# A hybrid decoder trunk on one core: the state-space sums moved behind the fifth step's value products, and a compression on two column groups

## The reference

```python
# NSA: overlapping blocks of 32 tokens, every 16, are compressed to one key and one value each
nc = S // CMP_STRIDE - 1                                   # 15 blocks
def compress(t, pe, w):
    ch = t.reshape(B, S // CMP_STRIDE, CMP_STRIDE, d)
    blk = jnp.concatenate([ch[:, :-1], ch[:, 1:]], axis=2)
    return ((blk + pe).reshape(B, nc, CMP_LEN * d) @ w).astype(F32)
kc = compress(keys[:, :, 0], cmp_pe[0], w_cmp[0])          # d = 64
vc = compress(vals[:, :, 0], cmp_pe[1], w_cmp[1])
# SSD: running sums of the decay within and over chunks of 128 tokens
a_cs = jnp.cumsum(a, axis=-1)
Lm = jnp.exp(segsum(a))
scores = jnp.einsum('bclhn,bcshn->bhcls', Cc, Bc) * Lm
y_diag = jnp.einsum('bhcls,bcshp->bclhp', scores, x)
```

## Time and profile before

| | us |
|---|---|
| median of three runs | 1509.21 (1509.17 to 1509.39) |
| the profiled execution, its own time | 1509.64 |
| its span in the trace | 1507.9 |
| TensorE busy | 1486.9 (99% of the span) |
| VectorE busy | 1213.4 (80%) |
| ScalarE busy | 1000.3 (66%) |
| mixers' loop, layer 0 / layer 1 | about 80 to 137 / 457 to 514 |

### The profile page before, as it was taken

One profiled execution on the slowest core, in us unless ns is written; L12 is line 12 of the kernel. 1 busy time (PEld: TensorE's weight loads), 2 busy tenths in 40 slices (PEclk: granted clock), 3 DMA queues, 4 the chain that ended last, 5 costly groups with the idle time before them and its releaser, 6 DMA issues.

```text
span 1507.9 us, 20053 instructions
## 1 busy us (share of the span) xinstructions
PE 1486.9 (99%) x7413; PEld 1245.8 (83%) x7413; DVE 1213.4 (80%) x1283; ACT 1000.3 (66%) x894; POOL 82.7 (5%) x126
## 2 busy tenths in 40 slices
PE   9999999999999999999999999999999999999997
PEld 7987888888898888888888888888888888888885
DVE  7778545545577899989898899898988899889986
ACT  7376543444547577787777777777777777778765
POOL 3102000000000110000000000000000000000000
PEclk9999999999999999999999999999999999999999
DMA  9705655555530379999999999999999999999992
GB/s 319 249 2 131 240 176 195 194 195 170 190 115 2 112 274 396 396 354 394 395 346 394 394 356 384 394 380 357 396 394 345 394 396 342 395 396 344 393 396 87
DMA packets 189980, 444.23 MB, mean 295 GB/s; under 512 B 9729, under 2 KB 16014, under 8 KB 189918
## 3 DMA queue, kind: packets, MB, share of 16 engines
q1 hardware_dynamic: 185366, 427.81, 77.5%
q0 software_dynamic: 4528, 15.58, 3.9%
q10 hardware_dynamic: 24, 0.01, 0.0%
HBM read 435.51 MB, written 7.86 MB: 294 GB/s over the span
## 4 chain that ended last, share of the span: by engine, by line
PE 94%; DVE 2%; ACT 2%; issue 1%; POOL 0%; SPq 0%; DMA 0%; POOLq 0%; DVEq 0%; ACTq 0%
PE bank L478 27%; PE bank L479 27%; PE bank L477 27%; PE bank L618 3%; PE bank L540 2%; PE bank L732 1%; PE bank L621 1%; PE bank L780 1%; PE bank L749 1%; PE bank L790 0%; PE bank L1020 0%; DMA ring<-in_w_in_dram 0%; POOL rstd L1303 0%; PE bank L650 0%; PE bank L713 0%
## 5 line engine op out<-in xcount | busy, mean ns | idle before, releaser
L1909 DVE TENSOR_TENSOR w_lo<-ring,w_hi 128x2048 fp32r<-128x2048 f32 x372 | 846.4, 2290 | 176.1 <-ACT w_hi L1427 175.6
L1427 ACT ACTIVATE w_hi<-ring 128x2048 fp32r<-128x2048 f32 x372 | 712.2, 1917 | 221.7 <-PE bank L477 221.7
L478 PE MATMUL bank<-w_hi,xT_hi 128*128 128x512 f32 x896 | 353.5, 395 | 0.0
L479 PE MATMUL bank<-w_hi,xT_lo 128*128 128x512 f32 x896 | 349.4, 390 | 0.0
L477 PE MATMUL bank<-w_lo,xT_hi 128*128 128x512 f32 x896 | 240.2, 390 | 0.0
L478 PE MATMUL bank<-w_hi,hidT_hi 128*128 128x512 f32 x560 | 220.6, 394 | 0.0
L479 PE MATMUL bank<-w_hi,hidT_lo 128*128 128x512 f32 x560 | 218.2, 390 | 0.0
L477 PEld LDWEIGHTS bank<-w_lo,xT_hi 128*128 128x128 f32 x896 | 168.1, 188 | 36.0 <-DVE w_lo L1909 0.3
L479 PEld LDWEIGHTS bank<-w_hi,xT_lo 128*128 128x128 f32 x896 | 168.3, 188 | 33.9
L478 PEld LDWEIGHTS bank<-w_hi,xT_hi 128*128 128x128 f32 x896 | 168.3, 188 | 33.6
L478 PE MATMUL bank<-w_hi,hT_hi 128*128 128x512 f32 (+2 forms) x384 | 147.3, 387 | 4.8 <-DVE hT_lo L1864 2.7
(11 more groups left out here) (393 smaller groups left out, 1269.6 us busy)
## 6 DMA issues: line engine op xcount, KB each, us to landing
ring<-in_moe_w_gate_dram SPq DMA_DIRECT2D x112, 1024.0 KB, 9.4
ring<-in_moe_w_up_dram SPq DMA_DIRECT2D x112, 1024.0 KB, 9.4
ring<-in_moe_w_down_dram SPq DMA_DIRECT2D x112, 1024.0 KB, 9.1
ring<-in_ffn_w_gate_dram SPq DMA_DIRECT2D x14, 1024.0 KB, 5.2
ring<-in_ffn_w_up_dram SPq DMA_DIRECT2D x14, 1024.0 KB, 5.1
ring<-in_ffn_w_down_dram SPq DMA_DIRECT2D x14, 1024.0 KB, 4.8
ring<-in_w_in_dram SPq DMA_DIRECT2D x11, 1024.0 KB, 5.3
ring<-in_w_out_dram SPq DMA_DIRECT2D x8, 1024.0 KB, 8.9
```

Of the source, the lines that this page charges most:

```text
L478: pe.matmul(o, x_hi, w, start=start, stop=False)
L479: return pe.matmul(o, x_lo, w, start=False, stop=False)
L1427: act.activation(w_hi[:, (base + at) % SPLIT, :], ring[:, i, :], ACT.Copy).then_inc(hi_ready, 1)
L1909: dve.tensor_tensor(w_lo[:, v, :], ring[:, (base + at) % RING, :], w_hi[:, v, :].bitcast(F32), ALU.subtract).then_inc(lo_ready, 1)
```

## The change

`compress` writes the keys' result to partitions 0 to 14 and the values' to 32 to 46, and takes them in turn for every j, where it made all 16 products of the keys before those of the values. VectorE copies `ckv` in two pieces. On TensorE `ssd_sums()` is called behind `products(2)` and `turn_probs(3)` in step n = 4; on VectorE the block of step n = 4 stands behind `outputs(2)`, and the block of n = 2, which stays ahead of `outputs(0)`, is only written further up.

```diff
-                    for c in range(2):
-                        for j in range(CLEN // 2):
-                            mm = pe.matmul(b[0:NC, c * HD:(c + 1) * HD], cin[:, j, c, :], w_cmp[:, j, c * HD:(c + 1) * HD],
-                                           start=(j == 0), stop=(j == CLEN // 2 - 1))
+                    for j in range(CLEN // 2):
+                        for c in range(2):
+                            mm = pe.matmul(b[32 * c:32 * c + NC, c * HD:(c + 1) * HD], cin[:, j, c, :],
+                                           w_cmp[:, j, c * HD:(c + 1) * HD], start=(j == 0), stop=(j == CLEN // 2 - 1))
...
-                    if n == 4:
-                        ssd_sums()
                     if n >= 2:
                         products(n - 2)
                     if n == 7:
                         turn_output(0)
                     if 1 <= n <= len(AJ):
                         turn_probs(n - 1)
+                    if n == 4:
+                        ssd_sums()
...
+                    if n == 2:
+                        b = filled()
+                        dve.tensor_copy(ckv[0:NC, 0:HD], b[0:NC, 0:HD])
+                        empty_bank(dve.tensor_copy(ckv[0:NC, HD:2 * HD], b[32:32 + NC, HD:2 * HD]))
+                        tell(conv(xbc, xraw, "scw", "scb", 6, 4, 6), "ssd_conv", ssd_conv)
+                    if 1 <= n <= len(AJ) and AJ[n - 1][0] == "cmp":
+                        mask_cmp(n - 1)
+                    if n >= 2 and n != 8:
+                        outputs(n - 2)
+
                     if n == 4:
 
                         b = filled()
...
-                    if n == 2:
-                        b = filled()
-                        empty_bank(dve.tensor_copy(ckv[0:NC, :], b[0:NC, 0:2 * HD]))
-                        tell(conv(xbc, xraw, "scw", "scb", 6, 4, 6), "ssd_conv", ssd_conv)
-                    if 1 <= n <= len(AJ) and AJ[n - 1][0] == "cmp":
-                        mask_cmp(n - 1)
-                    if n >= 2 and n != 8:
-                        outputs(n - 2)
```

## The result

| | median us | ratio to before, 95% interval |
|---|---|---|
| before | 1509.19 (4 runs) | |
| changed kernel | 1518.71 (1516.2 to 1519.3, 4 runs) | 1.0059 (1.0047 to 1.0070) |

Forecast was 1509.6 with a range to 1512.2. The time came out 9.5 us above before, outside the range, and its runs spread over 3.1 us where those of before spread over 0.4. The traced execution is the fastest of the four: it took 1516.2 us, its span is 1514.4, and its mean granted clock 0.994. In the other three that clock was 0.991 to 0.992.

A forecast was written before the change was run, and what follows sets the result against it. TensorE, busy 99% of the span, was taken as the bound. Per layer its gains and the new wait net 0.21 us later, twice +0.4, so 1509.6 us from a median of 1509.21; range 1508.6 to 1512.2.

The forecast's parts named there:

- Compression: TensorE's 64 compression records on two column groups stream side by side, about 1.9 us instead of 3.68 per layer.
- The dearer rival: In the compression each of 31 column-group changes drains the array, 0.10 to 0.13 us each: +8.7 to +10.5 us; chance 0.10.
- What g buys, and the wait: ScalarE's copy of probT(1) comes 1.04 us earlier and no more; TensorE then waits 2.6 us before products(2).
- g: TensorE time per layer gained in the compression by two column groups: 1.8 us taken, 0 or negative in rivals.
- The order, VectorE's block, the sum: Sums behind products(2): scores(5) 0.21 us later per layer; nobody waits for VectorE's moved block; +0.4 us in all.
- The sum: TensorE per layer: 1.8 + 0.65 + 0.05 us won, 2.6 lost waiting, 0.1 in products(2); 0.21 us later, twice.
- The clock falls in the new wait: Rival: the 2.6 us TensorE wait drops the clock to 1.2 GHz for the work behind it, +11 us; chance 0.04.
- the bad case: In the compression, issue times of loads and products add up to 0.05 us a record, leaving a gain of 0.5.

The follow-up runs named there:

- e7: Kernel before with the compression in two column groups, not alternating (all key products before those of the values), and the copy in two pieces, sums in their old place: 1509.10 us.
- e1: Changed kernel with five products of 256 columns of constants (2.2 us, result overwritten) filling the new wait in front of products(2): 1509.48 us.
- e8: Kernel before with only the sums moved, compression in one column group, and four products of constants (1.7 us) filling the wait: 1512.20 us.
- e3: Kernel before with only the sums moved behind products(2) and turned probabilities(3), compression in one column group, wait unfilled: 1517.87 us.
- e5: Changed kernel with one product of 256 columns of constants (0.43 us) in front of products(2): 1519.02 us.
- e6: Changed kernel with three products of 256 columns of constants (1.3 us) in front of products(2): 1510.10 us.
- e2: Kernel before with only the compression on two alternating column groups and the copy in two pieces, sums in their old place: 1506.99 us.

## Why the prediction was wrong

*Compression*: right. 1.90 us forecast and measured; e7 shows the mechanism. The dearer rival, a drain at each change of column group (+8.7 to +10.5), happened to give the measured time, 1518.7, by a mechanism that did not occur; without the profile after, the number would have seemed to confirm it. The rule of the Trainium skill ("TensorE: Matmul & The Clock Gate", Part 3, "What overlaps and what doesn't") by which a weight load runs under a product only for another row group does not hold here: 64 loads and products of the same rows ran in 1.90 us, and the loads alone, 0.09 us each, would take 5.8 one behind the other. The rule of the Trainium skill on modes and tiles (TensorEngine Tiling (Array Packing), "Key Properties") agrees with the 1.90 us.

*What g buys, and the wait*: right. ScalarE stood where the walk along its rows put it (probT(2) ready after 12.08 us for 12.12), and the wait was 2.58 for 2.6.

*The order, VectorE's block, the sum*: right at full clock. The sum gave +0.4 with g whole and +2.5 with g = 0; e1 measured -0.1 (1509.48 against 1509.58) and e8 +2.65. Layer by layer the traces are closer: +0.17 in e1 for 0.21, +1.24 in e8 for 1.25. Behind scores(5) nobody waits for the moved block: the next scores start 5.60 us later in e1 as in the kernel before.

*The clock*: this is the step that failed. The sum puts the work behind the new wait (products(2), turned probabilities(3), the sums) at full clock, and gives the rival "The clock falls in the new wait" 0.04. The ground was that an idle time of 1.35 had left the clock at its upper level. That row says nothing on 2.6, nearly twice as long, and I had written that down in the same sentence; the term was left out of the sum all the same. The runs showed that the clock does fall there, in both layers of the trace, and that this costs 9.2 us (e1 against the changed kernel's median; 9.6 with each against its own kernel before), where the prediction had +11 for it. In the traced run, the fastest of four, the low stretches are 3.4 and 10.2 us long and cost half of that, 6.8.

And there was a row, which I had not looked for. In the trace of the kernel before, TensorE's last instruction ends at 1499.6, and no work follows:

```profile
1499.60:1502.40 2.80, 0.02 (x1) 0.00 (x0) 2.03 (x6) 2.27 (x8) 0.57 (x1) 1.00 0.00 0
1502.43:1507.80 5.37, 0.00 (x0) 0.00 (x0) 2.05 (x3) 0.00 (x0) 0.99 (x1) 0.50 0.51 197
```

The clock fell 2.8 us after TensorE had stopped (2.1 to 5.1 us over the ten traces). It costs nothing there, but it is a fall after an idle time close to the forecast wait of 2.6, and it speaks against a chance of 0.04.

The waits of over 0.9 us in front of TensorE's work that the ten traces hold, behind its first instruction:

| idle us | kernel, place | granted clock behind it |
|---|---|---|
| 2.58 | changed, before products(2) | fell in both |
| 1.87 | e3, same place | fell in layer 0, not in layer 1 |
| 1.85, 1.86 | e5, same place | fell in both |
| 1.35 | all ten, start of the dense part and of layer 1 | stayed at 1.00, 20 of 20 |
| 1.14, 0.98, 0.97 | e8, e6, e3, in the input projection of layer 0 (L477) | stayed, 3 of 3 |
| 0.99 | e6, before products(2) | stayed in both |
| 0.95 | e2, in the sums | stayed in both |

What stays open: why the same 1.87 us cost the clock in one layer and not in the other, why a low stretch is 3.4, 6.8 or 10.2 us long, why the fall comes at so different a distance from the start of the wait (1.6 us in layer 0 of e5, 3.3 in layer 0 of e3), and whether it is the length of the pause alone or also the work on both sides that counts. No wait between 1.35 and 1.85 was tried.

## What to carry to other kernels

Where TensorE is the bound, a reordering is priced twice: the wait that it opens, and, when that wait is longer than any that the trace shows at full clock, the same work at half the clock behind it, here 7 us in the traced run and 9 in the median for a wait of 2.6 in each of two layers. Look for such a row over the whole trace, its end included, and not only in the part that the change touches. Work that stands "in the way" of a critical step may be the work that covers its wait; look what the step waits for before moving the cover behind it, and split the cover rather than move it whole. Two products with few output rows ran at once here when neighbours in the list went to different column groups.

## What the runs showed of the hardware

- Products of 15 output rows and 64 columns, one to partitions 0-14 and the next to 32-46: 64 records in 1.90 us, 0.030 each, against 0.0575 in one group (e7 in two groups but not alternating: 0.054). Issuing loads and products did not hold it to the 0.05 a record that the prediction had as the bad case.
- The clock can fall inside a wait or after TensorE has gone on: in e5 0.2 us before the end of the wait, in the changed kernel 0.3 behind it, in e3 1.4 behind it (layer 0 of all three). The row with the slow products need not be the one next to the wait.
- A wait filled with products whose result is overwritten cost nothing and kept the clock, here 9.2 us for ten instructions in two layers; three fillers did nearly as well as five (1510.1 and 1509.5).
- Median and spread belong together: each kernel whose clock stayed in its trace has its runs within 0.4 to 2.1 us (before among them), each whose clock fell within 3.1 to 4.7 (4 to 27 runs each).
